# First two column pairs of a feed-forward layer as eight block products each, in place of seven

## The chip, the core and the metric

The kernel runs on one core of a Trainium2 chip. The metric is the device time of one execution in microseconds (us). TensorE does the matmuls, ACT (ScalarE), DVE (VectorE) and POOL (GpSimd) the elementwise work, SP issues most DMAs.

## What is computed

Two blocks on 1024 tokens of width 1024 in float32. The change lies at the seam between the second block's last projection with its layer norm and the feed-forward layer behind it:

```python
h = layer_norm(DEEPNORM_ALPHA * h + m @ w_out[l], ln1_g[l], ln1_b[l])
f = jnp.square(jax.nn.relu(h @ w_ff1[l])) @ w_ff2[l]      # 1024 -> 4096 -> 1024
h = layer_norm(DEEPNORM_ALPHA * h + f, ln2_g[l], ln2_b[l])
```

## The kernel before

**Precision.** Each float32 operand is split in a high part (fp32r, copied by ACT) and a low part (operand less high part, by POOL for weights and the first operands, by DVE for the later ones). A block product is three products, high x high, high x low of the operand, low weight x high. Features lie on partitions, tokens along the free axis, in two halves of 512. The contraction of 1024 is eight tiles of 128, so a half of it is four tiles.

**Seven products.** Both feed-forward layers use Winograd's form of Strassen's method on 2 x 2 blocks. In the first layer the blocks of the operand are contraction half by token half (B11, B21 for tokens 0 to 511; B12, B22 for the others), the sums of them are T1 to T4; the weights of a *pair* n (two output tiles of 128) give seven factors, four of them sums. A *product* is 4 contraction tiles x 3 = 12 matmuls of 128x128 with 512 columns. There are FF_PAIRS = 16 pairs. `ORDER1` is the order of products, `G1` its inverse. From pair 2 on the seven products of a pair run one after the other into four PSUM banks of `pt`. The products of pairs 0 and 1 are interleaved, so that what needs only B11, B21 and B22 comes first, then T1, T3, T2, T4.

**Before the layer.** The last two output projection tiles run by token halves. Sums for the layer norm (`ln_sums`), the scalars of it on DVE (`ln_scale`), their spread to all partitions on TensorE (`ln_spread`, into the `wk` banks), then `normalise` on DVE (lines 1689 and 1690), `ln1` on ACT (line 999 scales into `yr`, line 1002 makes the high part) and `operand_lo` on POOL (line 558) make an operand tile. All 16 are made, 12 of them with parts. DVE's `operand_sum` (line 1701) and `operand_rest` (line 1707) make T1 to T4 and their low parts; ACT's `operand_hi` the high parts.

**Weights.** `weight_hi` (ACT, line 992) and `weight_lo` (POOL, line 551) fill four slots of `wr_h`, `wr_l` in product order; `first_sum` (POOL, line 568) makes the factor sums of pairs 0 and 1, `pair_sums` (DVE, from line 1751) those of later pairs.

**Outputs.** DVE adds products into the four output quarters, squares the rectified ones and makes the sums that the second layer wants, in `stg`; SP stores them in HBM. Each engine runs its own program in the order written, held by semaphores (`prod_done`, `wh_done`, `wl_done`, `bh_done`, `bl_done`, `tx_done`, `tl_done`).

Of the kernel before, what the change touches and what calls it, by code (L numbers as in the profile page):

```python
# [24 lines left out]
P = 128  # L25
# [54 lines left out]
ORDER1 = [(0, 1), (1, 1), (0, 2), (1, 2), (0, 3), (1, 3), (0, 5), (1, 5), (0, 7), (1, 7), (0, 6), (1, 6), (0, 4), (1, 4)]  # L80
ORDER1 += [(n, p) for n in range(2, FF_PAIRS) for p in (1, 6, 5, 7, 2, 3, 4)]
G1 = {np_: g for g, np_ in enumerate(ORDER1)}
FF1_PRODUCTS = len(ORDER1)
# [7 lines left out]
X_BASE, W_BASE, TH_BASE, XH_BASE, XL_BASE = 32, 16 * S_FF // 2, 12, 28, 16  # L91
B_SP, B_T1, B_XFREE, B_U2, B_S5, B_C22, B_C12, B_C21 = 3, 2, 2, 8, 8, 2, 3, 2 * C
S2_BASE, EV_BASE = 4 * (FF_PAIRS - 2), 6 * FF_PAIRS
# [23 lines left out]
def two_blocks_kernel(nc, xT, pT, ws, w_dt, w_low, vecs, dt_bias, a_log, b_low, w_gate2, b_gate,  # L117
# [110 lines left out]
    FXO = {"B11": R2, "B21": R2 + 16384, "B22": W0 + 8192, "T1": A0, "T3": A0 + 16384, "T2": A1, "T4": A1 + 16384}  # L228
# [19 lines left out]
    nrm = at("nrm", [2, HALF], ECo)  # L248

# [101 lines left out]
    sp_done, s_done = dt_b, sem("s_done")  # L351
# [21 lines left out]
    def _(sp):  # L373
# [41 lines left out]
        for q in range(2 * KT):  # L415
            h, k = divmod(q, KT)
            k = (k + 4 * h) % KT
            sp.wait_ge(h_done, q + 1)
            sp.dma_start(h_d[k, :, cols(h)], yr[:, k, cols(h)]).then_inc(h_put, 16)
        for n in range(2):  # L420
            sp.wait_ge(wl_done, G1[n, 4] + 1)
            pair_load(n + 2)

        for n in range(FF_PAIRS - 1):
            sp.wait_ge(st_done, 6 * n + 1)
            stage_put(n, "B22")
            if 2 <= n < FF_PAIRS - 2:
                sp.wait_ge(wl_done, G1[n, 4] + 1)
                pair_load(n + 2)
# [3 lines left out]
            sp.wait_ge(f11_done, n + 1)  # L433
            stage_put(n, "B11")
            for i, name in enumerate(STAGED[2:]):
                sp.wait_ge(st_done, 6 * n + 2 + i)
                stage_put(n, name)
# [4 lines left out]
        for e, p in enumerate((1, 6, 5)):  # L442
            sp.wait_ge(prod_done, G1[last, p] + 1)
            factor_load(e)
        sp.wait_ge(prod_done, G1[last, 7] + 1)
        block_load(0, 1)
        block_load(0, 2)
        sp.wait_ge(st_done, 6 * last + 1)
        stage_put(last, "B22")
        sp.wait_ge(prod_done, G1[last, 2] + 1)  # L450
        block_load(0, 3)
        sp.wait_ge(f11_done, last + 1)
        stage_put(last, "B11")
        for i, name in enumerate(STAGED[2:]):
            sp.wait_ge(st_done, 6 * last + 2 + i)
# [9 lines left out]
        sp.wait_ge(wl_done, FF1_PRODUCTS)  # L465
# [3 lines left out]
        for e in range(3, 7 * FF_BLOCKS):  # L469
# [3 lines left out]
            if i == 1 and 1 <= b < 3:  # L473
                for q in range(4):
                    sp.wait_ge(wl_done, FF1_PRODUCTS + 28 * (b - 1) + 25 + q)
# [10 lines left out]
    def _(pool):  # L486
# [57 lines left out]
        def weight_lo(g):  # L544
            if g < FF1_PRODUCTS:
                src = factor(*ORDER1[g])
            else:
                b, r = divmod(g - FF1_PRODUCTS, 28)
                src = factor2(b, r % 4, ORDER2[r // 4])
            pool.wait_ge(wh_done, g + 1)  # L550
            nc.gpsimd.tensor_tensor(out=wr_l[:, g % 4, :], in0=src, in1=wr_h[:, g % 4, :].bitcast(f32),  # L551
                                    op=ALU.subtract).then_inc(wl_done, 1)

        def operand_lo(i):
            name, k = ("B11", "B21", "B22")[i // 4], i % 4
            src = yr[:, k + (0, 4, 4)[i // 4], cols(i // 8)]
# [3 lines left out]

        def first_sum(n, i):

            r, s = fraw[n], fsum[n]
            out, x, y, op = ((s[:, 0, :], r[:, 1, 0, :], r[:, 1, 1, :], ALU.add), (s[:, 1, :], s[:, 0, :], r[:, 0, 0, :], ALU.subtract),
                             (r[:, 1, 0, :], r[:, 0, 0, :], r[:, 1, 0, :], ALU.subtract), (s[:, 2, :], r[:, 0, 1, :], s[:, 1, :], ALU.subtract))[i]
            if i:
                pool.wait_ge(sp_done, B_SP + 4 * n + i)
# [1902 lines left out]
```

## Time and profile before

| | |
|---|---|
| median of 3 runs | 2578.66 us (2574.72 to 2580.64) |
| profiled execution, its own time | 2576.28 us |
| its span, first to last instruction | 2574.6 us |
| mean granted TensorE clock | 0.976 of 2.4 GHz |
| last output projection starts its last matmul | 1848.97 us |
| pair 3 of the first layer starts | 1958.01 us |
| second feed-forward layer starts | 2208.2 us |

Times in the rows are us from the span's start. A matmul's duration holds its latency; the spacing of starts is its cost. "Idle before" is how long the engine stood still ahead of a row, and what ended it.

### The profile page before, as it was taken

The page shows a single profiled execution, that of the slowest core. Times are in us where ns is not written, and L with a number is a line of the kernel's source. Part 1 is how long each engine was busy: PE and PEld are TensorE (multiplying, and loading weights), DVE is VectorE, ACT ScalarE, POOL GpSimd, SP SyncE. Part 2 cuts the span into 40 slices and gives each one's busy share as a digit, 9 for nine tenths or more (in the row PEclk, how much of TensorE's full clock was granted, in tenths as well). Part 3 has the DMA queues.
Part 4 walks back from the last instruction along what each step waited for, and adds up shares of the span by engine and source line. Part 5 has one row for each costly group of instructions (what it writes and reads, how often), then busy time and mean ns, then how long its engine had stood idle before and what let it go on. Part 6 is the DMA issues. An engine that isn't in the chain of part 4 may idle for free. (4 is left out here: it accounts for less than half of the span.)

```text
span 2574.6 us, 34207 instructions
## 1 busy us (share of the span) xinstructions
PE 2442.9 (95%) x12938; PEld 1995.4 (78%) x12938; DVE 1497.8 (58%) x1961; ACT 734.8 (29%) x937; POOL 1064.0 (41%) x569
## 2 busy tenths in 40 slices
PE   7999999999999799999999999999879999999986
PEld 5778888887888588778877877888657888788865
DVE  6765565556611652123266676546767666766798
ACT  4332232222200211251022222222252333344333
POOL 4433343333444644233323233244465555456551
PEclk9999999998999999999999999999989999999997
DMA  5122122122111332122222222232124445844221
GB/s 199 44 65 74 65 81 77 61 83 89 49 49 43 106 105 67 46 102 82 82 83 63 75 79 64 78 100 65 58 82 162 165 135 163 323 163 151 96 82 66
DMA packets 100962, 246.05 MB, mean 96 GB/s; under 512 B 10849, under 2 KB 36705, under 8 KB 96242
## 3 DMA queue, kind: packets, MB, share of 16 engines
q1 hardware_dynamic: 59904, 186.67, 21.9%
q10 hardware_dynamic: 40946, 57.78, 6.6%
q8 instruction: 83, 1.36, 0.2%
q14 instruction: 29, 0.24, 0.0%
HBM read 183.53 MB, written 60.88 MB: 95 GB/s over the span
## 5 line engine op out<-in xcount | busy, mean ns | idle before, releaser
L500 POOL TENSOR_TENSOR w_hi<-w_raw,ones 128x1024 fp32r<-128x1024 f32 x139 | 269.4, 1938 | 1112.2 <-PE pt L1947 1061.5
L504 POOL TENSOR_TENSOR w_lo<-w_raw,w_hi 128x1024 fp32r<-128x1024 f32 x139 | 384.1, 2763 | 10.9
L1947 PE MATMUL pt<-xh,w_hi 128*128 128x512 f32 x976 | 306.6, 396 | 7.3 <-POOL w_lo L504 4.8
L1947 PE MATMUL pt<-xh,w_lo 128*128 128x512 f32 x976 | 302.4, 391 | 0.0
L1947 PE MATMUL pt<-h,w_hi 128*128 128x512 f32 x896 | 290.9, 406 | 5.5 <-ACT ea L930 3.7
L1947 PE MATMUL pt<-l,w_hi 128*128 128x512 f32 x896 | 277.9, 391 | 0.0
L1947 PE MATMUL pt<-h,w_lo 128*128 128x512 f32 x896 | 277.1, 390 | 0.0
L1947 PE MATMUL pt<-xl,w_hi 128*128 128x512 f32 x864 | 268.5, 392 | 0.0
L1947 PEld LDWEIGHTS pt<-xh,w_hi 128*128 128x128 f32 x976 | 183.1, 190 | 53.3 <-issue 15.6
L1947 PEld LDWEIGHTS pt<-xh,w_lo 128*128 128x128 f32 x976 | 184.4, 189 | 38.9
L1947 PEld LDWEIGHTS pt<-l,w_hi 128*128 128x128 f32 x896 | 168.8, 188 | 36.6
L1947 PEld LDWEIGHTS pt<-h,w_lo 128*128 128x128 f32 x896 | 168.5, 188 | 36.6
L1947 PEld LDWEIGHTS pt<-h,w_hi 128*128 128x128 f32 x896 | 160.2, 189 | 42.0 <-ACT ebuf L848 5.3
L1947 PEld LDWEIGHTS pt<-xl,w_hi 128*128 128x128 f32 x864 | 164.2, 190 | 34.9
L551 POOL TENSOR_TENSOR wr_l<-raw,wr_h 128x512 fp32r<-128x512 f32 x80 | 133.3, 1671 | 102.9 <-ACT wr_h L992 102.9
L551 POOL TENSOR_TENSOR wr_l<-fraw,wr_h 128x512 fp32r<-128x512 f32 x64 | 94.4, 1477 | 103.3 <-ACT wr_h L992 103.2
L551 POOL TENSOR_TENSOR wr_l<-fsum,wr_h 128x512 fp32r<-128x512 f32 x48 | 72.6, 1525 | 54.6 <-ACT wr_h L992 54.6
L992 ACT ACTIVATE wr_h<-raw 128x512 fp32r<-128x512 f32 x80 | 50.4, 632 | 129.1 <-PE pt L2338 102.7
L1385 DVE TENSOR_TENSOR acc_a<-acc_a,eb 128x1024 f32<-128x1024 f32 x6 | 20.1, 3344 | 95.6 <-ACT eb L767 95.6
L992 ACT ACTIVATE wr_h<-fraw 128x512 fp32r<-128x512 f32 x64 | 39.9, 629 | 104.8 <-PE pt L2338 90.2
L1874 DVE TENSOR_TENSOR yr<-yr,pt 128x512 f32<-128x512 f32 x64 | 43.4, 681 | 44.9 <-PE pt L2338 44.9
L2338 PE MATMUL pt<-xs0h,wr_h 128*128 128x512 f32 x144 | 57.8, 401 | 6.3 <-issue 6.3
(494 smaller groups left out, 5008.1 us busy)
## 6 DMA issues: line engine op xcount, KB each, us to landing
w_raw<-ws_d SPq DMA_DIRECT2D x140, 512.0 KB, 3.6
fx_d<-stg SPq DMA_DIRECT2D x112, 256.0 KB, 2.8
fraw<-ws_d SPq DMA_DIRECT2D x32, 512.0 KB, 4.8
raw<-ws_d SPq DMA_DIRECT2D x32, 512.0 KB, 8.6
xs0f<-fx_d SPq DMA_DIRECT2D x10, 1024.0 KB, 4.8
xs1f<-fx_d SPq DMA_DIRECT2D x9, 1024.0 KB, 4.8
xs2f<-fx_d SPq DMA_DIRECT2D x9, 1024.0 KB, 4.8
x_raw<-xT_d SPq DMA_DIRECT2D x32, 256.0 KB, 7.1
```

What stands on the lines that cost most here:

```text
L500: nc.gpsimd.tensor_tensor(out=w_hi[:, u, :], in0=w_raw[:, u, :], in1=zeros, op=ALU.add).then_inc(w_hi_done, 1)
L504: nc.gpsimd.tensor_tensor(out=w_lo[:, u, :], in0=w_raw[:, u, :], in1=w_hi[:, u, :].bitcast(f32), op=ALU.subtract).then_inc(w_split, 1)
L551: nc.gpsimd.tensor_tensor(out=wr_l[:, g % 4, :], in0=src, in1=wr_h[:, g % 4, :].bitcast(f32), op=ALU.subtract).then_inc(wl_done, 1)
L992: A(wr_h[:, g % 4, :], src, ACT.Copy).then_inc(wh_done, 1)
L1385: TT(out=acc_a[:], in0=acc_a[:], in1=eb[:], op=ALU.add).then_inc(sq_used, 1)
L1874: ins = TT(out=y, in0=y, in1=bank(q), op=ALU.add)
L1947: ins = MM(pt[:, slot, h * HALF:(h + 1) * HALF], wt[:, w, k * P:(k + 1) * P], x[:, k, h * HALF:(h + 1) * HALF], start=first and k == 0 and ...
L2338: ins = MM(out, wt[:, g % 4, k * P:(k + 1) * P], xx[:, k, :], start=first and k == 0 and n == 0, stop=k == 3 and n == 2, skip_group_check= ...
```

## The change

Pairs 0 and 1 no longer use the seven products. Each output quarter is computed plainly: two block products, eight a pair, 16 in all. The token halves are taken one after the other. `PLAIN` numbers the eight weight blocks (pair n, output tile m, contraction half k). The first four are in the ring slots, the second four in the place of T4's operand, and all eight stay there for both halves. In the first half TensorE takes an operand tile of B11 and multiplies it with all four first weights before it takes the next; then come the four others with B21. The second half does the same for two banks of `wk` at a time, which hold the spread layer norm scalars until the normalisation is over. B12 becomes an operand (in T2's place), so all 16 operand tiles get a low part on POOL. ACT rectifies the finished quarters out of PSUM and squares them; DVE makes the sums for the second layer later. DVE normalises all eight tiles of the first half before the scalars of the second, and makes all T1 and T3 sums behind the last normalisation, in one run; T2 and T4 wait for the plain products. Pair 2 has an order of its own, and the loads of pairs 2 and 3 are issued between the stores of the normalised tiles. The diff at its core (counters that only shift are left out):

```diff
-ORDER1 = [(0, 1), (1, 1), (0, 2), (1, 2), (0, 3), (1, 3), (0, 5), (1, 5), (0, 7), (1, 7), (0, 6), (1, 6), (0, 4), (1, 4)]
-ORDER1 += [(n, p) for n in range(2, FF_PAIRS) for p in (1, 6, 5, 7, 2, 3, 4)]
-G1 = {np_: g for g, np_ in enumerate(ORDER1)}
-FF1_PRODUCTS = len(ORDER1)
+PLAIN = [(n, m, k) for k in range(2) for m in range(2) for n in range(2)]
+ORDER1 = [(n, p) for n in range(2, FF_PAIRS) for p in ((1, 5, 7, 6, 2, 3, 4) if n == 2 else (1, 6, 5, 7, 2, 3, 4))]
+G1 = {np_: len(PLAIN) + g for g, np_ in enumerate(ORDER1)}
+FF1_WEIGHTS = len(PLAIN) + len(ORDER1)
+LEAD = 4
+FF1_PRODUCTS = FF1_WEIGHTS + LEAD
...
+           "B12": A1}
...
+    def plain(w):
+
+        n, m, k = PLAIN[w]
+        return fraw[n][:, m, k, :]
+
+    def weight_slot(g):
+
+        return (wr_h[:, g % 4, :], wr_l[:, g % 4, :]) if not 4 <= g < 8 else (fx["T4"][0][:, g - 4, :], fx["T4"][1][:, g - 4, :])
+
+    def wk_bank(w):
+
+        return wk[:, (0, 2, 1, 3)[w % 4], :]
 
...
+            if q in (11, 13):
+                sp.wait_ge(wl_done, len(PLAIN) - 1 + (q - 11) // 2)
+                pair_load(2 + (q - 11) // 2)
...
-            sp.wait_ge(st_done, 6 * n + 1)
+            sp.wait_ge(f11_done, 4 * n + 1)
             stage_put(n, "B22")
-            if 2 <= n < FF_PAIRS - 2:
+            sp.wait_ge(f11_done, 4 * n + 2)
+            stage_put(n, "B11")
+            for i, name in enumerate(("T3", "T1", "T2")):
+                sp.wait_ge(st_done, 4 * n + 1 + i)
+                stage_put(n, name)
+            sp.wait_ge(f11_done, 4 * n + 4)
+            stage_put(n, "B21")
+            sp.wait_ge(st_done, 4 * n + 4)
...
         for g in range(4):
             weight_lo(g)
         operand_lo(0)
         operand_lo(1)
-        pool.wait_ge(y_done, KT)
-        pool.wait_ge(fr_in[0], W_BASE + 32)
-        first_sum(0, 0)
-        first_sum(0, 1)
+        weight_lo(4)
+        weight_lo(5)
         operand_lo(2)
         operand_lo(3)
-        first_sum(0, 2)
-        first_sum(0, 3)
-        for i in range(4, 8):
+        weight_lo(6)
+        pool.wait_ge(y_done, KT)
+        operand_lo(4)
+        weight_lo(7)
+        for i in range(5, 16):
             operand_lo(i)
-        weight_lo(4)
-        pool.wait_ge(stat_done, 7)
-        pool.wait_ge(fr_in[1], W_BASE + 32)
-        first_sum(1, 0)
-        first_sum(1, 1)
-        operand_lo(8)
-        operand_lo(9)
-        first_sum(1, 2)
-        first_sum(1, 3)
-        operand_lo(10)
-        operand_lo(11)
-        for g in range(5, FF1_PRODUCTS + 28 * FF_BLOCKS):
+        for g in range(8, FF1_WEIGHTS + 28 * FF_BLOCKS):
...
-                n, p = ORDER1[g]
+            if g >= 8:
+                act.wait_ge(prod_done, (5, 6, 9, 10)[g - 8] if g < 12 else g - 3 + LEAD)
...
+        def rectified(w):
+
+            return (r11[w % 2][:], t1[:, w % 2, :], u2[:, w % 2, :], s5[:, w % 2, :])[w // 2]
+
+        def plain_relu(w):
+
+            act.wait_ge(prod_done, (1, 2, 3, 4, 7, 8, 11, 12)[w])
+            A(rectified(w), bank(w) if w < 4 else wk_bank(w), ACT.Relu).then_inc(x_free, 1)
+
+        def plain_square(n, quarter):
+
+            act.wait_ge(x_free, B_XFREE + 8)
+            src = rectified(2 * quarter + n)
+            A(src if quarter == 2 else stg[:, n, {3: 0, 0: 1, 1: 5}[quarter], :], src, ACT.Square).then_inc(f11_done, 1)
+
...
-        for q in range(2, 5):
+        act.wait_ge(mm_done, S_FF)
+        for g in range(4, 8):
+            weight_hi(g)
+        for q in range(2, 12):
             ln1(q)
         act.wait_ge(y_done, KT)
-        first_product(0)
-        ln1(5)
-        ln1(6)
-        first_product(1)
-        ln1(7)
-        weight_hi(4)
-        act.wait_ge(mm_done, S_FF)
-        ln1(8)
-        ln1(9)
-        relu(0)
-        ln1(10)
-        ln1(11)
-        weight_hi(5)
+        act.wait_ge(stat_done, 7)
+        plain_relu(0)
         ln1(12)
-        act.wait_ge(stat_done, 7)
-        relu(1)
+        plain_relu(1)
         ln1(13)
-        weight_hi(6)
+        plain_relu(2)
         ln1(14)
-        operand_hi(0)
+        plain_relu(3)
         ln1(15)
-        weight_hi(7)
-        for i in range(1, 8):
+        for i in range(4):
             operand_hi(i)
-        weight_hi(8)
-        weight_hi(9)
-        for i in range(8, 12):
+        for g in range(8, 10):
+            weight_hi(g)
+        act.wait_ge(a_used, KT)
+        for i in range(4, 8):
             operand_hi(i)
-        weight_hi(10)
-        for i in range(12, 16):
+        plain_relu(4)
+        plain_relu(5)
+        for g in range(10, 12):
+            weight_hi(g)
+        for i in range(8, 14):
             operand_hi(i)
-        for g in range(11, 14):
-            weight_hi(g)
+        plain_relu(6)
+        operand_hi(14)
+        plain_relu(7)
+        operand_hi(15)
+        weight_hi(12)
         act.wait_ge(tx_done, 16)
-        act.wait_ge(bl_done, 12)
+        act.wait_ge(bl_done, 16)
         act.wait_ge(h_put, X_BASE + 16 * 2 * KT)
-        square_11(0)
-        square_11(1)
-        for g in range(14, 17):
-            weight_hi(g)
+        for n in range(2):
+            for quarter in (3, 0, 2, 1):
+                plain_square(n, quarter)
...
-                dve.wait_ge(h_done, 12 + k + 1)
-            if i // 4 >= 2:
+            if i // 4 < 2:
+                dve.wait_ge(h_done, 9 + i)
+            else:
                 dve.wait_ge(tx_done, i - 3)
+                dve.wait_ge(prod_done, (10, (7, 8, 11, 12)[k])[i // 4 - 2])
             TT(out=tf[name][:, k, :], in0=x, in1=y, op=op).then_inc(tx_done, 1)
...
         last_y(1, 1)
-        normalise(2, nrm, 0, 6)
-        normalise(3, nrm, 0, 6)
+        for q in range(2, KT):
+            normalise(q, nrm, 0, 6)
         ln_scale(1, 6)
-        for q in range(4, 14):
+        for q in range(KT, 2 * KT):
             normalise(q, nrm, 0, 6)
         dve.wait_ge(mm_done, S_FF)
-        operand_sum(0)
-        normalise(14, nrm, 0, 6)
-        operand_sum(1)
-        normalise(15, nrm, 0, 6)
-        operand_sum(2)
-        operand_sum(3)
-        operand_sum(4)
-        operand_sum(5)
-        operand_rest(0)
-        operand_rest(1)
-        operand_sum(6)
-        operand_rest(2)
-        operand_sum(7)
-        operand_rest(3)
+        for i in range(8):
+            operand_sum(i)
+        for k in range(4):
+            operand_rest(k)
+
...
+        dve.wait_ge(x_free, B_XFREE + 8)
         for n in range(2):
-            out_u2(n)
-            out_s5(n)
-            out_22(n)
-        pair_sums(2)
-        for n in range(2):
-            square_22(n)
-            out_12(n)
-            out_21(n)
+            dve.wait_ge(f11_done, 4 * n + 3)
+            operand_sums(n, u2[:, n, :], 4 * n)
+            dve.wait_ge(f11_done, 4 * n + 4)
+            last_operand(n, 4 * n + 3)
...
+        def plain_step(out, g, x, k, first, last):
+
+            w = weight_slot(g)
+            for n, (wt, xx) in enumerate(((w[0], x[0]), (w[0], x[1]), (w[1], x[0]))):
+                ins = MM(out, wt[:, k * P:(k + 1) * P], xx[:, k, :], start=first and n == 0, stop=last and n == 2)
+            return ins
+
+        pe.wait_ge(evac_done, N_FF - 1)
+        for k in range(4):
+            pe.wait_ge(bl_done, k + 1)
+            for g in range(4):
+                if k == 0:
+                    pe.wait_ge(wl_done, g + 1)
+                    if g == 2:
+                        pe.wait_ge(evac_done, N_FF)
+                plain_step(bank(g), g, fx["B11"], k, k == 0, False)
             if k == 1:
                 ln_sums(1, (a_used, KT))
-            if k == 3:
+        for g in range(4, 8):
+            pe.wait_ge(wl_done, g + 1)
+            for k in range(4):
+                pe.wait_ge(bl_done, 4 + k + 1)
+                ins = plain_step(bank(g - 4), g, fx["B21"], k, False, k == 3)
+            ins.then_inc(prod_done, 1)
+            if g == 6:
                 ln_spread(1, 8)
-
-        pe.wait_ge(evac_done, N_FF - 1)
-        product(bank(0), 0, fx["B11"], True, False, (bl_done, 0), in_first)
-        product(bank(1), 1, fx["B11"], True, False, (bl_done, 0))
+        for m in range(2):
+            pe.wait_ge(ln_done, (KT, 2 * KT)[m])
+            for half, base in (("B12", 8), ("B22", 12)):
+                second = half == "B22"
+                for k in range(4):
+                    pe.wait_ge(bl_done, base + k + 1)
+                    for n in range(2):
+                        g = 2 * m + n
+                        ins = plain_step(wk_bank(g), g + 4 * second, fx[half], k, not second and k == 0, second and k == 3)
+                        if k == 3:
+                            ins.then_inc(prod_done, 1)
+
+        g = G1[2, 1]
+        pe.wait_ge(x_free, B_XFREE + 1)
+        product(bank(0), g, fx["B11"], True, False)
+        pe.wait_ge(x_free, B_XFREE + 3)
+        product(bank(2), g + 1, fx["T1"], True, False, (tl_done, 0))
+        pe.wait_ge(x_free, B_XFREE + 4)
+        product(bank(3), g + 2, fx["T3"], True, False, (tl_done, 4))
+        product(bank(1), g + 3, fx["T2"], True, True, (tl_done, 8))
         pe.wait_ge(t1_done, B_T1 + 1)
-        product(bank(0), 2, fx["B21"], False, False, (bl_done, 4))
-        pe.wait_ge(t1_done, B_T1 + 2)
-        product(bank(1), 3, fx["B21"], False, False, (bl_done, 4))
-        pe.wait_ge(evac_done, N_FF)
-        product(bank(2), 4, fx["B22"], True, True, (bl_done, 8))
-        product(bank(3), 5, fx["B22"], True, True, (bl_done, 8))
-        pe.wait_ge(ln_done, 2 * KT)
-        product(wk[:, 0, :], 6, fx["T1"], True, True, (tl_done, 0))
-        product(wk[:, 1, :], 7, fx["T1"], True, True, (tl_done, 0))
-        product(wk[:, 2, :], 8, fx["T3"], True, False, (tl_done, 4))
-        product(wk[:, 3, :], 9, fx["T3"], True, False, (tl_done, 4))
-        pe.wait_ge(x_free, B_XFREE + 1)
-        product(bank(0), 10, fx["T2"], True, True, (tl_done, 8))
-        pe.wait_ge(x_free, B_XFREE + 2)
-        product(bank(1), 11, fx["T2"], True, True, (tl_done, 8))
+        product(bank(0), g + 4, fx["B21"], False, False)
+        pe.wait_ge(s5_done, B_S5 + 1)
+        product(bank(2), g + 5, fx["B22"], False, False)
         pe.wait_ge(c22_done, B_C22 + 1)
-        product(wk[:, 2, :], 12, fx["T4"], False, False, (tl_done, 12))
-        pe.wait_ge(c22_done, B_C22 + 2)
-        product(wk[:, 3, :], 13, fx["T4"], False, False, (tl_done, 12))
-
-        for n in range(2, FF_PAIRS):
-            g = 7 * n
-            pe.wait_ge(*((u2_done, B_U2 + 1) if n == 2 else (x_free, B_XFREE + n)))
+        product(bank(3), g + 6, fx["T4"], False, False, (tl_done, 12))
+
...
```

## Rows read from the trace of the kernel before

**Rows 1.** The page's first part: busy time and share of each engine.

```profile
PE 2442.9 (95%) x12938; PEld 1995.4 (78%) x12938; DVE 1497.8 (58%) x1961; ACT 734.8 (29%) x937; POOL 1064.0 (41%) x569
```

**Rows 2.** Windows: us, busy time of engines, granted clock (PEclk), DMA.

```profile
1849.20:1958.00 108.80, 78.33 (x285) 59.92 (x285) 82.76 (x120) 45.42 (x74) 65.67 (x40) 0.81 0.29 104
...
1958.00:2208.20 250.20, 247.69 (x1094) 204.80 (x1092) 156.68 (x204) 81.68 (x132) 126.26 (x92) 1.00 0.50 171
```

**Rows 3.** Timeline of TensorE: start, us, line, tiles, idle before and releaser.

```profile
1843.88 2.05 PE L2014 MATMUL wk<-ident,sm 128*128 128x128 f32 x16 [1.49 <-DVE sm L1679]
...
1848.97 0.39 PE L1963 MATMUL pt<-mh,w_lo 128*128 128x512 f32 x1
1850.87 0.47 PE L2338 MATMUL pt<-B11h,wr_h 128*128 128x512 f32 x1 [1.50 <-POOL B11l L558]
...
1857.13 1.84 PE L2009 MATMUL wk<-ones,acc_b 128*128 128x1 f32 x8
...
1932.29 0.39 PE L2338 MATMUL pt<-B11h,wr_h 128*128 128x512 f32 x1
...
1940.22 0.39 PE L2338 MATMUL pt<-T1h,wr_l 128*128 128x512 f32 x1
...
1958.01 0.39 PE L2338 MATMUL pt<-B11h,wr_h 128*128 128x512 f32 x1
```

**Rows 4.** Waits of TensorE, 1849.2 to 1958: sum, times, longest.

```profile
PE wk L2338 <- POOL wr_l L551: 8.6, 1, 8.6
...
PE pt L2338 <- DVE stg L1794: 4.3, 1, 4.3
...
PE pt L2338 <- POOL wr_l L551: 0.4, 1, 0.4
```

**Rows 5.** Windows at low clock, columns as in Rows 2.

```profile
1856.00:1866.00 10.00, 6.68 (x23) 5.24 (x24) 8.38 (x21) 2.78 (x4) 5.51 (x5) 0.50 0.14 52
...
1913.00:1918.30 5.30, 5.25 (x12) 4.13 (x13) 0.00 (x0) 0.00 (x0) 3.71 (x3) 0.50 0.00 0
```

**Rows 6.** Timeline of POOL around the change.

```profile
1858.25 2.64 POOL L558 TENSOR_TENSOR B11l<-yr,B11h 128x512 fp32r<-128x512 f32 x2 [1.78 <-ACT B11h L1002]
1860.85 1.27 POOL L568 TENSOR_TENSOR fraw<-fraw 128x512 f32<-128x512 f32 x1
...
1900.49 13.74 POOL L551 TENSOR_TENSOR wr_l<-fraw,wr_h 128x512 fp32r<-128x512 f32 x2 [5.43 <-ACT wr_h L992]
```

**Rows 7.** Timeline of ACT around the change.

```profile
1835.72 2.17 ACT L992 ACTIVATE wr_h<-fraw 128x512 fp32r<-128x512 f32 x4
...
1875.19 0.80 ACT L999 ACTIVATE yr<-nrm,vec 128x512 f32<-128x512 f32 x1
...
1876.56 0.80 ACT L999 ACTIVATE yr<-nrm,vec 128x512 f32<-128x512 f32 x1
```

**Rows 8.** Timeline of DVE around the change.

```profile
1855.27 0.68 DVE L1689 TENSOR_TENSOR nrm<-yr,wk 128x512 f32<-128x512 f32 x1
...
1856.58 0.68 DVE L1689 TENSOR_TENSOR nrm<-yr,wk 128x512 f32<-128x512 f32 x1
...
1859.01 0.16 DVE L1674 TENSOR_SCALAR sm<-wk 128x4 f32<-128x4 f32 x1 [1.03 <-PE wk L2009]
...
1860.95 1.20 DVE L1145 TENSOR_SCALAR sm<-sm 128x4 int32<-128x4 int32 x1
...
1865.18 0.68 DVE L1689 TENSOR_TENSOR nrm<-yr,wk 128x512 f32<-128x512 f32 x1
...
1886.61 1.49 DVE L1701 TENSOR_TENSOR T1f<-yr 128x512 f32<-128x512 f32 x1 [4.51 <-ACT yr L999]
...
1899.75 0.68 DVE L1701 TENSOR_TENSOR T2f<-T3f,yr 128x512 f32<-128x512 f32 x1
...
1909.38 2.49 DVE L1707 TENSOR_TENSOR T4l<-T4f,T4h 128x512 fp32r<-128x512 f32 x4
```

**Rows 9.** POOL's low weight parts (line 551): duration ns min/median/max.

```profile
L551 POOL TENSOR_TENSOR wr_l<-fraw,wr_h x64: 1265/1293/12502, 1836.4 to 2195.6; 128x512 fp32r<-128x512 f32 x64
```

## What the change will do to the time

> **What bounds the kernel now.** I read the page first: TensorE is busy for 95% of the span [rows 1], so only two things can move the end: the number of matmuls, and the holes between them. Next the stages. From pair 3 on the first layer has no holes worth naming: 13 pairs of 84 matmuls, 1092, take 250.2 us, 0.229 each at a granted clock of 1.00. The stretch ahead of it, from the last output projection at 1849.2 to pair 3 at 1958.0, takes 108.8 us at a mean clock of 0.81 [rows 2]. It holds 14 products of the first two pairs and seven of pair 2, 252 matmuls. Back to back a matmul starts every 0.227 us (36 of them, 35 steps in 7.93 us [rows 3]), so these are 57 us of work. The nine rows of what TensorE waited for there sum to 30.6 us, the largest being 8.6 for a low weight part from POOL [rows 4]; two sums and a spread of the layer norm take some 7 more. The rest is mostly low clock: 0.50 in two windows shown, where 12 matmuls take 5.30 us, 0.44 each against 0.227, thus 0.21 more per matmul [rows 5]. Everything after 1958.0 is fed from there and moves with it. So the question is how many us pass between 1849.2 and the first matmul of pair 3.
>
> **The work that is added and taken.** 14 products of 12 matmuls become 16: 24 more matmuls, 24 x 0.227 = +5.4 us. The weight sums of the two pairs (eight POOL operations) go. DVE's five combining additions and three squarings a pair go to ACT, as four rectifications and four squares. Four B12 operands come, one copy on ACT and one subtraction on POOL each. Bare work of the stretch is now 276 x 0.227 = 62.7 us.
>
> **First token half.** ACT, POOL and DVE are unchanged up to the first operand, which lets TensorE in at 1850.87 [rows 3]. There an operand tile fed three matmuls (0.7 us); now it feeds four weights, 12 matmuls, 2.7 us. Tile 2 lands near 1853.1, so TensorE runs from 1850.9 to 1856.3. The sums stood at 1857.1 + 1.8 at low clock [rows 3]; I take 1.9 for both, to 1858.2. Tile 3 is ready at 1859.5 (POOL did tiles 3 and 4 in 2.64 us from 1858.25, [rows 6]): hole of 1.4, then tiles 3 and 4 to 1865.0. ACT makes a normalised tile and its high copy every 1.37 us (1875.19 to 1876.56, [rows 7]), DVE's normalisation takes 1.31 (1855.27 to 1856.58, [rows 8]) and POOL 1.3 a tile. Behind tile 4 POOL also has two weights' low parts, so tiles 5 to 8 land at 1863.5, 1866.1, 1867.4 and 1868.7; the fifth weight's product follows them and ends at 1869.5, the sixth and seventh at 1874.9. The four extra weight copies on ACT cost 2.2 us (2.17 for four, [rows 7]) and lie at 1852.7 to 1854.9, where ACT waited until 1856.7 anyway: free. The scalars of the second half took from 1859.01 to 1865.18, 6.2 us [rows 8]. They now start after the normalisation of tile 8, near 1863.5, and are done by 1871: hidden under the products, where the old order stopped TensorE. The spread (2.05 us, [rows 3]) goes to 1876.8, the eighth product to 1879.5. Against the old trace the second half's normalisation is late: it starts at 1876.9.
>
> **Second token half.** DVE 1.4, ACT 1.4 and POOL 1.3 in line put the first B12 operand at 1881.1, a hole of 1.6. Each operand now feeds two weights, six matmuls, 1.36 us, against a pace of 1.4 on ACT, 1.9 where four rectifications (half a us each, from ACT's 0.54 a copy) are woven in. So operands 9 to 14 are ready at 1881.1, 1882.5, 1883.9, 1885.3, 1887.2 and 1889.1, and TensorE has used them at 1890.4.
>
> **The new wait.** Here DVE finishes the last normalisation, near 1888.6, and goes straight on to the T1 and T3 sums and four remainders: 12 additions with both inputs in SBUF, 0.60 to 0.62 each (2.49 for four, [rows 8]), without a wait that bites, to 1896.3, then the four weight sums of pair 2. POOL gets operand 15 from ACT at 1889.7. What happens then the old trace shows: POOL's low part at 1900.49 took 12.5 of the 13.74 us of two operations and ended only after DVE's run of additions (1899.75 shown, last one over at 1911.87) [rows 6, 8, 9]. The other way round, a DVE addition that began beside a running POOL operation took 1.49 in place of 0.68. Where each DVE operation waits for its forerunner POOL does get in: it worked back to back beside the scalar chain, and a DVE step there took 1.20 [rows 6, 8]. So I let POOL in at the first self-wait of the weight sums, 1897.0: operand 15 at 1898.3, operand 16 at 1901.4. TensorE stands still from 1890.4 to 1898.4, 8 us; such holes left it at clock 0.50 for 5.3 us after [rows 5], 12 matmuls x 0.21 = +2.6, and 0.6 waiting for operand 16. It ends operand 16 at 1903.9. The second two weights of each pair, 48 matmuls, follow without a wait, to 1914.8. Bounds of this wait: none, if POOL gets in between two DVE additions; the old 12.5 us at most.
>
> The Trainium skill (SBUF — State Buffer, Who interferes with whom) says that a DVE instruction with two SBUF inputs contends with a GpSimd instruction that reads SBUF, and that whoever issues first holds the shared pair for the whole instruction. Read as a lock of one instruction, POOL would lose one addition and get in; the 12.5 us row differs, since POOL lost a whole run there. By the page the sum would be that of rival B.
>
> **Pair 2.** T2 can only be written when B12 is used up, at 1909.4 (24 matmuls before 1914.8). From there DVE runs 20 additions, 20 x 0.60 = 12.1 us, and then eight operand sums of the plain pairs. The third and fourth weights of pair 2 reach ACT at 1908.7 and 1909.4 too, since their slots hold plain weights until then. Their low parts queue on POOL in the moment when DVE starts: again starved. First two products of pair 2 run to 1920.2; the third has its weight at 1922.1 if POOL won the first race, at 1924.2 if not. I take a hole of 3.3 and 1.9 for the clock after it. Seven products are 84 x 0.227 = 19.05. End of pair 2: 1914.8 + 19.05 + 5.2 = 1939.1. DVE's eight sums end by 1931, the second-layer stores of pair 0 leave in time for staging slot 0, and pair 3 finds its waits met. SP issues the same 16 stores of normalised tiles, now with the loads of pairs 2 and 3 between them, some 40 us earlier than before; the stores behind them are next needed by ACT's squares after 1918. The eight squares (0.54 each) wait until DVE has read the last tile, about 1918.5, and are over at 1923; queued behind them on ACT is pair 2's next weight copy, wanted by TensorE at 1930.
>
> **Sum.** 62.7 matmuls, 3.7 sums and spread, holes 1.6 + 1.4 + 1.7 (tiles 6 to 8 and the step to them) + 1.6 + 1.0 (pace of operands 9 to 14) + 8.6 + 3.3, low clock 2.6 + 1.9: 90.1, against 108.8. Gain 19. From the profiled 2576.3 (span 2574.6) this gives 2557.3; the median shown is 2.4 higher, and I say 2558. A difference below 0.2%, 5 us, could not be told from none.
>
> **Rivals.**
> **A**, the forecast, 0.60; own range 2551 to 2565.
> **B**, POOL is not starved: operand 16 at 1892.9, its matmuls to 1894.3, plain products to 1905.2, pair 2 to 1924.3. Gain 34, 2543. For it: the scalar chain, and the margin is thin, operand 15 misses DVE's start by 1 us. Against it: the 12.5 us row. 0.15. It decides between; an operand 15 that slips in alone gains only 1, as 16 still waits.
> **C**, low clock in the first half: in the old trace it was 0.50 from 1856 to 1866, with sums and short bursts as here [rows 5]. If it holds from 1856 through the spread, 60 matmuls x 0.21 less what covers waits, the spread comes 7 to 12 us later: 2565 to 2570. Against it: TensorE has 24 matmuls before 1856, where it had ten. 0.17.
> **D**, slower: the clock stays at 1.2 GHz throughout the paced stretch, because operands arrive one by one. 252 matmuls x 0.44 + 24 x 0.227 + 7 of sums + 3 us of holes = 126 against 108.8, +18, 2595. It decides when some 90 more matmuls than forecast run low (19 / 0.21). Against: 1.00 from 1873 on in runs as dense. 0.05. The last 0.03 are for a wait I have not seen that eats the gain.
>
> **Range.** 2543 to 2569 leaves out D and the far part of C. Faster 0.92, same 0.03, slower 0.05.
>
> **What would show it.** POOL's subtraction for the third B22 tile several times 1.3 us, ending after DVE's run; TensorE's largest waits in the stretch for that tile and for a low weight of pair 2; no wait for the spread's scalars; pair 3 starting near 1939; the same 250 us after it. Wrong would be a spread well after 1877, or a clock of 0.5 over more than 15 us.

## The result: 17 us less where 19 were forecast

The changed kernel took 2560.51 us (median of 4 runs, 2557.74 to 2562.72), the kernel before 2577.94 on the same chip (4 runs, 2574.72 to 2580.64). The ratio is 0.9927, 95% interval 0.9912 to 0.9941: 15 to 23 us less. The profiled execution took 2562.72, with a span of 2560.5. The prediction said 2558, from 2543 to 2569.

The windows of the changed kernel, columns as in [rows 2]:

```profile
1856.10:1942.40 86.30, 73.39 (x309) 58.09 (x309) 75.74 (x102) 48.14 (x82) 44.72 (x30) 0.94 0.37 130
1942.40:2192.60 250.20, 247.70 (x1093) 204.77 (x1091) 157.18 (x205) 81.65 (x132) 125.70 (x91) 1.00 0.50 171
1866.50:1870.00 3.50, 3.47 (x9) 2.73 (x10) 3.40 (x6) 3.40 (x6) 3.43 (x3) 0.55 0.50 183
1928.50:1931.40 2.90, 2.90 (x8) 1.98 (x6) 2.90 (x2) 0.15 (x1) 2.90 (x3) 0.50 1.04 374
1935.40:1938.30 2.90, 2.90 (x7) 2.32 (x8) 2.83 (x5) 0.05 (x1) 0.00 (x0) 0.50 0.50 172
```

The stretch that the prediction speaks of begins with the last projection matmul and ends with pair 3. It is 86.3 us in place of 108.8 in these windows, its granted clock 0.94 in place of 0.81 [rows 2], and the 13 pairs behind it take 250.2 us as before. Three short times at low clock are left, where 15 us and more had it before. By starts of matmuls, which I use from here on, the stretch is 86.6 us (1855.87 to 1942.42), against 109.0 (1848.97 to 1958.01, [rows 3]). TensorE's own timeline:

```profile
1855.87 0.39 PE L1982 MATMUL pt<-mh,w_lo 128*128 128x512 f32 x1
1857.70 0.47 PE L2368 MATMUL pt<-B11h,wr_h 128*128 128x512 f32 x1 [1.44 <-ACT ea L972]
...
1881.85 1.95 PE L2033 MATMUL wk<-ident,sm 128*128 128x128 f32 x16
...
1888.26 0.47 PE L2368 MATMUL wk<-B12h,wr_h 128*128 128x512 f32 x1 [1.71 <-POOL B12l L588]
...
1912.38 0.39 PE L2357 MATMUL pt<-B11h,wr_h 128*128 128x512 f32 x1
...
1927.14 0.50 PE L2357 MATMUL pt<-B21h,wr_h 128*128 128x512 f32 x1 [3.72 <-ACT t L1041]
...
1935.37 0.80 PE L2357 MATMUL pt<-B22h,wr_h 128*128 128x512 f32 x1 [3.63 <-DVE s L1772]
...
1942.42 0.39 PE L2357 MATMUL pt<-B11h,wr_h 128*128 128x512 f32 x1
```

Two of the stretch's holes stand here, each ahead of a product of pair 2. All that TensorE waited for in the stretch, in the wait view, is 12.6 us, where it was 30.6 [rows 4]:

```profile
PE pt L2357 <- ACT t L1041: 3.7, 1, 3.7
PE pt L2357 <- DVE s L1772: 3.6, 1, 3.6
PE wk L2368 <- POOL B12l L588: 1.7, 1, 1.7
...
PE pt L2368 <- ACT ea L972: 1.4, 1, 1.4
PE pt L2368 <- POOL B11l L588: 1.4, 1, 1.4
PE wk L2368 <- POOL B22l L588: 0.8, 2, 0.6
```

L2368 is the plain step, L2357 a product of seven; L588 is `operand_lo`, L582 `weight_lo`, L1041 the copy t of pair 2's first product, L1772 the sum s5. Nothing is left of the waits for a low weight part and for T1. The largest two are new and belong to pair 2.

The stretch is 22.5 us shorter in the two profiles (109.04 to 86.55), but the whole span only 14.1 (17.4 by the medians of the times). Of the missing 8.4 us, 6.9 lie ahead of the stretch, where the last projection came later in this profile, and 1.5 behind it, which is within what repeats of one kernel differ there. The first two experiments look into the 6.9.

### The profile page after: what moved, and what is told of

The parts are those of the page before. It is cut to its first block and busy times, and to the rows that moved or that the text cites. A ratio compares the mean times of both kernels' runs of the same rounds, so it can differ in the third digit from the quotient of the medians.

```text
span 2560.5 us, 34221 instructions
## 1 busy us (share of the span) xinstructions
PE 2441.9 (95%) x12962; PEld 1995.1 (78%) x12962; DVE 1495.0 (58%) x1945; ACT 737.5 (29%) x945; POOL 1045.8 (41%) x559
## 5 line engine op out<-in xcount | busy, mean ns | idle before, releaser
L582 POOL TENSOR_TENSOR wr_l<-raw,wr_h 128x512 fp32r<-128x512 f32 x80 | 133.6, 1673 | 103.4 <-ACT wr_h L1004 103.4
L582 POOL TENSOR_TENSOR wr_l<-fraw,wr_h 128x512 fp32r<-128x512 f32 x60 | 81.0, 1353 | 93.0 <-ACT wr_h L1004 93.0
L582 POOL TENSOR_TENSOR wr_l<-fsum,wr_h 128x512 fp32r<-128x512 f32 x42 | 64.2, 1538 | 57.4 <-ACT wr_h L1004 57.3
L2357 PE MATMUL pt<-xs0h,wr_h 128*128 128x512 f32 x144 | 57.4, 399 | 7.0 <-issue 7.0
L910 ACT ACTIVATE darg<-darg 128x512 f32<-128x512 f32 x56 | 34.9, 630 | 99.3 <-DVE darg L1556 98.9
```

The costliest lines, as they stand in the source:

```text
L582: nc.gpsimd.tensor_tensor(out=low, in0=src, in1=high.bitcast(f32), op=ALU.subtract).then_inc(wl_done, 1)
L910: A(darg[:, n % 2, :, :], darg[:, n % 2, :, :], ACT.Exp).then_inc(lev_exp, 1)
L2357: ins = MM(out, wt[:, g % 4, k * P:(k + 1) * P], xx[:, k, :], start=first and k == 0 and n == 0, stop=k == 3 and n == 2, skip_group_check= ...
```

## The experiments

Stretch is counted as above in each profile. Ratios are against runs of the kernel before on the same chip.

| kernel | last projection at, us | stretch, us | ratio to before (95%) |
|---|---|---|---|
| before / again | 1848.97 / 1849.13 | 109.0 / 107.3 | |
| changed / again | 1855.87 / 1859.75 | 86.6 / 87.9 | 0.9927 (0.9912 to 0.9941) |
| before_breath | 1850.26 | 101.6 | 0.9967 (0.9953 to 0.9981) |
| scalars_early | 1855.81 | 93.3 | 0.9941 (0.9925 to 0.9958) |
| weight_outer | 1851.26 | 92.6 | 0.9936 (0.9919 to 0.9953) |
| shorter_tail | 1848.88 | 86.4 | 0.9914 (0.9896 to 0.9932) |
| longer_half | 1856.40 | 92.1 | 0.9946 (0.9931 to 0.9962) |
| sums_between / again | 1854.21 / 1854.25 | 81.9 / 82.1 | 0.9899 (0.9880 to 0.9917) / 0.9893 (0.9874 to 0.9912) |
| both_moved | 1859.86 | 83.5 | 0.9903 (0.9885 to 0.9922) |
| all_moved | 1851.55 | 82.9 | 0.9905 (0.9886 to 0.9923) |

**Both kernels again.** Expected of the kernel before:

> The kernel before, profiled again. Stretch means from the start of the last projection matmul to the first matmul of pair 3: 109.0 us in the first profile of before (1848.97 to 1958.01), 86.6 in that of the changed kernel (1855.87 to 1942.42). The two profiles also differ ahead of the stretch, by 6.9 us. Theory: the lead-in differs by chance, through the clock granted early in the program, so this profile may start the stretch anywhere from 1848 to 1856, while the stretch itself repeats to 1 us, with POOL's 12.5 us subtraction in it again. Rival: the change itself makes the lead-in longer, then this one starts at 1849 again. Second rival: the 12.5 us subtraction is a chance event; then it is missing here and the stretch is 7 to 10 us shorter.

and of the changed one:

> The changed kernel, profiled again. Theory: stretch 86.6 us to within 1, holes of 3.7 and 3.6 us in pair 2 again, lead-in anywhere from 1848 to 1856. Rival: the lead-in of 1855.9 belongs to the change and repeats.

The kernel before started its stretch at 1849.1 and kept it to 1.7 us, and POOL's long subtraction is there to the nanosecond. The view by line and form, as in [rows 9]:

```profile
L551 POOL TENSOR_TENSOR wr_l<-fraw,wr_h x64: 1265/1293/12502, 1836.6 to 2194.0; 128x512 fp32r<-128x512 f32 x64
```

The changed kernel's stretch repeated to 1.4 us; the end of its lead-in (all that is ahead of the stretch) came out at 1859.8, later than the 1856 that was expected at most. The holes of pair 2 were 3.7 and 2.8 us. The instructions ahead of the stretch are the same in all these kernels. Comparing the same ACT instruction over the profiles, the differences arise as steps: 5 to 6 us between 155 and 270 us in the second profile of the changed kernel, 4 to 5 us near 1500 in its first. Over the 13 profiles the lead-in lies from 1849 to 1860, and a changed kernel (shorter_tail) had the lowest. But the three profiles without the change all lie below 1851, and seven of the ten with it above 1854, so I can't say that the change has no part in it; no run here settles that. The stretch is the sharper measure, as it repeated to 0.2 to 1.7 us where the times of one kernel lie 2 to 11 us apart.

**The starved subtraction.** In the kernel before, DVE's run got a wait of each operation for the one ahead:

```diff
         for k in range(4):
             operand_sum(8 + k)
+            dve.wait_ge(tx_done, 8 + k + 1)
             operand_rest(4 + k)
+            dve.wait_ge(tl_done, 4 + k + 1)
...
             operand_sum(12 + k)
+            dve.wait_ge(tx_done, 12 + k + 1)
             operand_rest(8 + k)
+            dve.wait_ge(tl_done, 8 + k + 1)
```

> The kernel before, with one edit: in DVE's run of T2 and T4 additions and the low parts between them (16 operations) each one waits for the one ahead of it. Theory, POOL is starved by additions of DVE that follow each other without a gap: POOL gets in at once, its 12.5 us subtraction falls below 2 us, TensorE's wait of 8.6 us for that weight goes to 0 to 2 us, DVE's run takes 2 us more for the waits and up to 4 for POOL's turns; the stretch becomes 100 to 105 us instead of 109. Rival, the long subtraction has another cause (an operand of its own or a load): it stays above 10 us and the stretch is 109 to 112.

POOL's timeline, then DVE's, in this kernel:

```profile
1900.71 3.53 POOL L551 TENSOR_TENSOR wr_l<-fraw,wr_h 128x512 fp32r<-128x512 f32 x2 [5.42 <-ACT wr_h L992]
```

```profile
1900.68 0.69 DVE L1707 TENSOR_TENSOR T3l<-T3f,T3h 128x512 fp32r<-128x512 f32 x1
1901.41 1.67 DVE L1701 TENSOR_TENSOR T2f<-T3f,yr 128x512 f32<-128x512 f32 x1
1903.11 1.67 DVE L1707 TENSOR_TENSOR T3l<-T3f,T3h 128x512 fp32r<-128x512 f32 x1
```

Two subtractions of POOL now take 3.53 us together in place of 13.74 [rows 6]. DVE's steps stand 0.72 us apart in place of 0.60 where POOL is idle, and 1.70 where it lets POOL in. TensorE's wait of 8.6 for the weight is gone; what is new is 3.5 us for a quarter out of DVE, whose run is longer:

```profile
PE wk L2342 <- DVE stg L1778: 3.5, 1, 3.5
```

The stretch fell to 101.6, as expected. So waits between DVE's operations let POOL in at this place: this is shown. That a run without them shuts POOL out wherever it stands is not. The waits also moved the moment of POOL's request, 0.02 us into a DVE operation in place of 0.14, and no run changes one without the other. The kernel is also 0.33% (0.19 to 0.47) faster for four added waits in the source.

**The scalars put back.** The changed kernel, with DVE's scalars of the second half ahead of tiles 5 to 8 again:

```diff
-        for q in range(2, KT):
+        for q in range(2, 4):
             normalise(q, nrm, 0, 6)
         ln_scale(1, 6)
-        for q in range(KT, 2 * KT):
+        for q in range(4, 2 * KT):
```

> The changed kernel, with DVE's scalars of the second half's layer norm back behind the fourth normalisation, as before the change, ahead of tiles 5 to 8. Theory: the move of these 6 to 7 us of DVE work was one source of the gain; the fifth operand tile comes 6 us later, TensorE waits 4 to 5 us for it behind the fourth, and the stretch is 91 to 94 us instead of 86.6. Rival: the product work of the first half hides it all, the stretch stays 86.6 to 88.

```profile
PE pt L2357 <- DVE s L1772: 3.9, 1, 3.9
PE pt L2357 <- ACT t L1041: 3.7, 1, 3.7
PE pt L2368 <- POOL B21l L588: 3.2, 2, 1.8
```

The third row is new: 3.2 us for B21 tiles, less than the 4 to 5 expected. The granted clock up to the spread was 0.84 in place of 0.93, and low clock took most of the rest. The stretch is 93.3, 5.4 to 6.7 us more. The time is 2566.0, by the ratios 0.14% more than the changed kernel, which the intervals don't separate; the stretch does.

**One weight at a time.** The four first weights one after the other over the B11 tiles:

```diff
-        for k in range(4):
-            pe.wait_ge(bl_done, k + 1)
-            for g in range(4):
...
+        for g in range(4):
+            pe.wait_ge(wl_done, g + 1)
...
+            for k in range(4):
+                if g == 0:
+                    pe.wait_ge(bl_done, k + 1)
+                plain_step(bank(g), g, fx["B11"], k, k == 0, False)
```

> The changed kernel, but in the first token half the four first weights are taken one after the other over the four B11 tiles, as products were before, in place of one tile for all four weights. The first weight then meets each tile as it lands and the other three come behind it. Theory: 36 matmuls that filled the waits for tiles 2 to 4 are done after them, the first half ends 3 to 5 us later, stretch 90 to 92 us instead of 86.6. Rival: TensorE has slack enough before the spread, stretch 86.6 to 88.

```profile
PE pt L2368 <- POOL B11l L588: 3.5, 3, 1.5
```

```profile
1881.88 1.95 PE L2033 MATMUL wk<-ident,sm 128*128 128x128 f32 x16
```

The waits for B11 tiles are 3.5 us, the old figure of the kernel before, in place of 1.4, and the granted clock up to the spread was 0.83 in place of 0.93. The spread (second fence) starts 30.6 us behind the last projection, where it was 26.0 and 27.2 in the two profiles of the changed kernel. The stretch is 92.6, 4.7 to 6.0 more.

**Matmuls left out behind B12.**

```diff
-                for k in range(4):
+                for k in range(3 if m == 1 and second else 0, 4):
                     pe.wait_ge(bl_done, base + k + 1)
```

> The changed kernel with 18 matmuls left out: of the second token half of the second output tile of both pairs, contraction tiles 4 to 6 are not multiplied (part of the result is missing). They are the last work of TensorE ahead of pair 2, 4.1 us. Theory A, these extra products are hidden: pair 2 waits for the rectified copy t behind eight squares on ACT, and for s5 behind eight sums on DVE, and that chain starts when B12 is used up, ahead of these matmuls; stretch 85 to 87 us as in the changed kernel, with longer holes in pair 2. Theory B, matmuls decide: stretch 82.5 us, 4.1 less.

```profile
PE pt L2357 <- ACT t L1041: 4.3, 1, 4.3
PE pt L2357 <- DVE s L1772: 3.2, 1, 3.2
...
PE pt L2357 <- DVE T2l L1730: 1.0, 4, 0.3
PE pt L2357 <- DVE T3l L1730: 0.9, 2, 0.6
```

```profile
1927.65 0.69 DVE L1772 TENSOR_TENSOR s<-pt,u 128x512 f32<-128x512 f32 x1
```

18 matmuls, 4.1 us, are gone, and the stretch is 86.4: nothing gained. Pair 2 starts 4.1 us earlier and takes 4.0 more. About half of that is waits (t 4.3 in place of 3.7, T2 and T3 1.9 where they had none, s5 3.2 in place of 3.6), the rest a lower clock, granted 0.85 in pair 2 in place of 0.89. DVE starts s5 (second fence) 78.8 us behind the last projection, and so it does in the first profile of the changed kernel (1934.62). The total is 2557.7, 2.8 below the changed kernel's median, with a lead-in that was 7 us shorter in the profile. Theory A holds: DVE's and ACT's chain, not the matmuls beside it, sets when pair 3 starts.

**Matmuls added ahead of the spread.**

```diff
-            for k in range(4):
+            steps = (0, 1, 2, 3) if g in (4, 7) else (0, 1, 2, 3, 0, 1, 2, 3)
+            for i, k in enumerate(steps):
                 pe.wait_ge(bl_done, 4 + k + 1)
-                ins = plain_step(bank(g - 4), g, fx["B21"], k, False, k == 3)
+                ins = plain_step(bank(g - 4), g, fx["B21"], k, False, i == len(steps) - 1)
```

> The changed kernel with 24 matmuls more: the sixth and seventh products of the first token half go twice over their four B21 tiles (so that part of the result is counted twice). This is the number that the change adds, put where TensorE works without a hole ahead of the spread. Theory: a matmul ahead of the spread costs its full 0.227 us, since the second half's normalisation and all behind it wait for the spread; stretch 92 us, 5.4 more than the 86.6 of the changed kernel. With the 18 matmuls that were free when left out behind B12, this says where the added products are paid. Rival: the waits of the second half for ACT and POOL take it up, stretch 86.6 to 89.

The stretch is 92.1: 24 matmuls more cost 5.6 against the first profile, 4.2 against the second, and 24 x 0.227 is 5.4. A matmul ahead of the spread is paid in full, one of the 18 behind B12 is free.

**The holes of pair 2.** DVE makes u2 and s5 of pair 2 before the sums of pair 1:

```diff
         for n in range(2):
+            if n == 1:
+                out_u2(2)
+                out_s5(2)
             dve.wait_ge(f11_done, 4 * n + 3)
             operand_sums(n, u2[:, n, :], 4 * n)
```

> The changed kernel, with DVE making u2 and s5 of pair 2 after the second-layer sums of pair 0 and ahead of those of pair 1. Theory: the second hole in pair 2 (3.6 us, for s5) and the low clock behind it go, stretch 81 to 83.5 us, 0.12 to 0.2% faster than the changed kernel. Rival: ACT or POOL is as late, the hole stays or moves to the next product, stretch 85 to 87.

> The kernel with u2 and s5 of pair 2 between the sums of pairs 0 and 1, once more on this chip. Theory: stretch 81.9 us to within 1, ratio to before 0.988 to 0.992. The lead-in before the stretch again lands anywhere from 1849 to 1860.

```profile
PE pt L2361 <- ACT t L1041: 3.7, 1, 3.7
```

The wait for s5 is gone, with the low clock behind it: stretch 81.9 and 82.1. Time 2555.67 and 2551.77, ratios 0.9899 and 0.9893: the fastest here, 1.0% below the kernel before. By these ratios they are 0.3% below the changed kernel; the two were not run side by side.

Then ACT's copy t ahead of the eight squares, with the rectified second quarters in another buffer, and last the sixth weight and the first output quarter of pair 2 earlier too:

```diff
-            return (r11[w % 2][:], t1[:, w % 2, :], u2[:, w % 2, :], s5[:, w % 2, :])[w // 2]
+            return (r11[w % 2][:], fsum[1][:, w % 2, :], u2[:, w % 2, :], s5[:, w % 2, :])[w // 2]
...
         weight_hi(12)
+        first_product(2)
         act.wait_ge(tx_done, 16)
```

```diff
+        first_product(2)
+        weight_hi(13)
...
             operand_sums(n, u2[:, n, :], 4 * n)
+            if n == 1:
+                out_22(2)
             dve.wait_ge(f11_done, 4 * n + 4)
```

> As the one before, and ACT copies pair 2's first product out ahead of the eight squares (the rectified second quarter of pairs 0 and 1 lies in an unused sum buffer, so that t is free). Theory: both holes go, but s5 is then wanted 4 us earlier, behind the low parts of T4 and the sums of pair 0 on DVE; one hole of 3 to 4 us stays. Stretch 79 to 82 us. Rival: the second hole only grows by what the first loses, and the stretch equals that of the kernel with the sums moved alone, within 0.5 us.

> As the kernel with both moves, and two steps more: ACT makes the sixth weight of pair 2 ahead of the eight squares, and DVE makes the first output quarter of pair 2 between the sums of pair 1 and its last one. In the kernel with both moves TensorE waited 2.1 us for that weight's low part, 2.3 us for that quarter and 1.0 us for s5. Theory: the first two shrink to at most 1 us, stretch 79 to 81.5 us against 83.5 and against 81.9 of the kernel with the sums between. Rival: the quarter waits for the stores of pair 0, which come no earlier, and the hole stays: 81.5 to 84.

The waits of the kernel with both moves:

```profile
PE pt L2362 <- DVE stg L1780: 2.3, 1, 2.3
PE pt L2362 <- POOL wr_l L582: 2.1, 1, 2.1
...
PE pt L2362 <- DVE s L1773: 1.0, 1, 1.0
```

The wait for t went and three others came, 5.4 us for 3.7: stretch 83.5, above the theory's 79 to 82 and above the rival's 81.4 to 82.4 too. With all moves it is 82.9, above the theory's 79 to 81.5. It is in the rival's range, but not by the rival's cause: the wait for the quarter is gone, and those for the weight and s5 stay. Neither is shorter than with the sums alone. TensorE's holes with all moves, and POOL's lines:

```profile
1921.24 0.47 PE L2366 MATMUL pt<-B21h,wr_h 128*128 128x512 f32 x1 [2.14 <-POOL wr_l L582]
...
1927.20 0.72 PE L2366 MATMUL pt<-B22h,wr_h 128*128 128x512 f32 x1 [2.99 <-DVE s L1775]
```

```profile
1918.22 2.88 POOL L582 TENSOR_TENSOR wr_l<-fraw,wr_h 128x512 fp32r<-128x512 f32 x1 [7.83 <-ACT wr_h L1004]
1921.06 1.74 POOL L582 TENSOR_TENSOR wr_l<-fsum,wr_h 128x512 fp32r<-128x512 f32 x1
```

The weight that TensorE waits for at 1921.24 is POOL's first line: this low part took 2.88 us in place of 1.27, shut out by DVE's four T4 remainders. With the sums alone it was as slow, but hidden behind the later t. The second line is the low part of the sixth weight, moved ahead; it now runs beside DVE's sums of pair 0, and s5 is ready 75.6 us behind the last projection, where it was 73.6 with the sums alone and 73.7 with both moves. In total time these two can't be told from the kernel with the sums alone.

## Why the prediction was right, and where it was not

**First half: right in its times.** Shifted by the lead-in's 6.9 us, I had tiles 5 to 8 at 1870.4, 1873.0, 1874.3 and 1875.6; POOL finished them at 1870.4, 1872.9, 1874.1 and 1875.4. The spread began the second normalisation at 1883.8, as forecast (1876.9 + 6.9), the first B12 operand entered at 1888.3 (forecast 1888.0). That the reuse of a tile for four weights and the scalars moved behind tile 8 fill the old holes is borne out by weight_outer (4.7 to 6.0 us) and scalars_early (5.4 to 6.7 us), each by undoing it alone. The fresh ACT and POOL work was hidden, as costed. Two terms of the sum had each other's place, though, which is luck: the hole of 1.7 for tiles 6 to 8 did not come, and low clock, put at nothing, took 1.7 (nine steps of 0.36 to 0.43 us in place of 0.23, in the window that begins at 1866.50). In the second profile the low clock lasted 6 us, and the spread came 1.2 us later.

**The step that failed: "So I let POOL in at the first self-wait of the weight sums, 1897.0".** Here are POOL's and DVE's timelines of the changed kernel:

```profile
1896.50 3.45 POOL L588 TENSOR_TENSOR B22l<-yr,B22h 128x512 fp32r<-128x512 f32 x2 [0.55 <-ACT B22h L1012]
1901.76 1.69 POOL L582 TENSOR_TENSOR wr_l<-fraw,wr_h 128x512 fp32r<-128x512 f32 x1 [1.81 <-ACT wr_h L1004]
...
1911.38 1.62 POOL L582 TENSOR_TENSOR wr_l<-fraw,wr_h 128x512 fp32r<-128x512 f32 x1 [1.89 <-ACT wr_h L1004]
1912.95 1.73 POOL L582 TENSOR_TENSOR wr_l<-fsum,wr_h 128x512 fp32r<-128x512 f32 x1
1922.53 2.87 POOL L582 TENSOR_TENSOR wr_l<-fraw,wr_h 128x512 fp32r<-128x512 f32 x1 [7.84 <-ACT wr_h L1004]
```

```profile
1895.34 5.15 DVE L1724 TENSOR_TENSOR T1f<-yr 128x512 f32<-128x512 f32 x4
...
1909.96 0.68 DVE L1724 TENSOR_TENSOR T2f<-T3f,yr 128x512 f32<-128x512 f32 x1
...
1911.77 1.78 DVE L1730 TENSOR_TENSOR T3l<-T3f,T3h 128x512 fp32r<-128x512 f32 x1
...
1921.79 2.48 DVE L1730 TENSOR_TENSOR T4l<-T4f,T4h 128x512 fp32r<-128x512 f32 x4
...
1933.23 0.69 DVE L1798 TENSOR_TENSOR stg<-stg 128x512 f32<-128x512 f32 x1
1933.84 0.68 DVE L1767 TENSOR_TENSOR u<-pt,t 128x512 f32<-128x512 f32 x1
1934.62 0.69 DVE L1772 TENSOR_TENSOR s<-pt,u 128x512 f32<-128x512 f32 x1
```

POOL asked at 1896.50, 1.2 us into DVE's run of T1 and T3 sums, and was let in behind the addition then running. Four T1 sums took 5.15 us in place of 2.4. Operands 15 and 16 were ready at 1898.2 and 1899.9, 7 and 8 us before my times, the hole of 8 us and its low clock (2.6) did not come, and pair 2 started 9.3 us earlier than forecast, lead-in taken off. That was rival B's mechanism, to which I had given 0.15; it had the plain products end at 1905.2, and they ended at 1905.5 with the lead-in taken off. I had carried one row [rows 9] over to another run of DVE. The row is true of its place (both profiles of the kernel before show it), but not a rule. The old trace held the warning, a low weight part that started beside the T1 and T3 sums and lost nothing:

```profile
1893.79 1.27 POOL L551 TENSOR_TENSOR wr_l<-fsum,wr_h 128x512 fp32r<-128x512 f32 x1 [3.32 <-ACT wr_h L992]
```

The Trainium skill (SBUF — State Buffer, Who interferes with whom) says that whoever issues first gets the shared pair for the whole instruction, and that issue order decides who blocks. Of POOL's five lines above, the first four agree with it: 1.60 to 1.74 us an operation, one addition's rest and then 1.3. The request at 1922.53 doesn't: 2.87 us, let in only when DVE's run of four T4 remainders was over. Nor does the 12.5 us one.

**The term that was missing: pair 2.** I had it at 24.3 us, 19.05 of work and 5.2 for one hole behind a starved weight with its clock. That weight was on time (1.62 us on POOL at 1911.38). But pair 2 took 30.0 us (1912.38 to 1942.42), with holes of 3.7 and 3.6 us. The prediction followed the copy of the next weight behind ACT's eight squares and saw that it was in time; it passed over the copy t, which is ahead of that weight in the same queue and wanted earlier. ACT's timeline:

```profile
1922.35 0.62 ACT L1032 ACTIVATE stg<-s 128x512 f32<-128x512 f32 x1
...
1926.51 0.58 ACT L1041 ACTIVATE t<-pt 128x512 f32<-128x512 f32 x1
```

The squares wait for DVE's last reading of the tile buffer, so t comes 3.7 us late. Likewise s5 stands behind eight sums; I never asked what TensorE wants in between. I had their end 16 us behind the start of pair 2 (1931 against 1914.8), and it was 21.5 (1933.9 against 1912.4). The 5.7 missing us are 7.3 of holes in place of 3.3, and 3.7 of low clock behind them (30.0 less 19.05 and 7.3; the last two windows at the top) in place of 1.9.

The sum had a second term wrong here, and it is the other side of the first: POOL's turns cost DVE time. I let T2 wait for B12 to be used up. TensorE was through with B12 at 1907.1, but DVE came to T2 only at 1909.96, as it had been busy without a gap since 1895.34 (TensorE's last matmul with B12, then the window with columns as in [rows 2]):

```profile
1906.71 0.39 PE L2368 MATMUL wk<-B12h,wr_l 128*128 128x512 f32 x1
```

```profile
1895.30:1924.30 29.00, 27.24 (x117) 21.23 (x115) 28.94 (x37) 18.54 (x34) 12.43 (x8) 1.00 0.22 81
```

These 36 additions would be 22 us at 0.60; six steps in them are 1.7 us, each with a turn of POOL, which is 6.6 more. The last 20 took 14.3 us (1909.96 to 1924.27) where I had 12.1. shorter_tail shows that this chain, and not the matmuls beside it, sets pair 3's start.

**Sum.** 9.3 us too much ahead of pair 2 and 5.7 too little in it: 90.1 forecast with its parts, 86.6 measured. The total came out at 2560.5 and not lower because the lead-in ended later, by 6.9 us in this profile. So the total is near the forecast partly by luck: two misses in the stretch ran against each other, and a later lead-in, which I had not reckoned with, took up what they left.

**The other rivals.** C fell: low clock held from 1866.5 to 1870.0 only, where I feared it to the spread. D fell with it, though my argument against it read the old trace too well: its granted clock is 1.00 from 1873 to 1885, but 0.90 over 1873 to 1900. The 24 extra matmuls were priced right as work (longer_half), but the last 18 of the stretch's plain products cost nothing.

**What stays open.** weight_outer and scalars_early account for 10 to 13 us of a gain of 19 to 22 in the stretch, each from its own undoing. Both moves, and the waits of before_breath, might be had with seven products too. No run has them there, so what the eight products are worth by themselves is not shown.

## What to carry to other kernels

When a change moves work behind an engine's queue, list every result that comes out of that queue with the time at which its reader wants it; the first one checked that is in time says nothing about the one ahead of it. At a seam between stages, put what each arriving tile can feed ahead of fewer operations: here the order by tiles was worth 4.7 to 6.0 us, about what 24 extra matmuls cost. An engine that is let in takes its turns from another: follow the cost to that one. A long stall seen once on a shared port is a fact of that place; bound it from both sides elsewhere.

## What the runs showed of the hardware

A POOL subtraction beside a gapless run of two-input DVE additions is usually let in after the one that runs, and DVE then takes 1.7 to 1.8 us for a step of 0.6. In two places it was shut out for the whole run instead, 12.50 us in both profiles of the kernel before and 2.87 to 2.88 in all ten of the kernels with the change. Both times the request came 0.14 us into a subtraction that makes a low part; a request 0.14 us into a T3 sum (1901.76) was let in. In the kernel before, a wait of each DVE operation for the last, 0.12 us a step, let POOL in behind one operation. What decides between the two cases is open: no run moves the request alone.
